# Five more weight pairs by seven block products, and the last expert group in halves of the columns

## The reference

```python
# layer 1
u = rms_norm(h, norm_pre_mix)
proj = u @ w_in                                   # 17 slabs of 512 columns
y_a = hgrn2_mixer(hq, hf, hi, hg, ...)            # gated linear recurrence
y_b = nsa_mixer(nq, kc, vc, ks, vs, kw, vw, ...)  # attention in three branches
merged = sigmoid(ga) * (y_a @ w_branch_a) + sigmoid(gb) * (y_b @ w_branch_b)
h = h + rms_norm(merged @ w_out)
h = h + rms_norm(square(relu(rms_norm(h) @ w_up)) @ w_down)
h = h + rms_norm((p @ w_ple) * sigmoid(h @ w_ple_gate))
# layer 2: two kinds of sparse attention, then 32 experts, 2 for each token
x = x + mixed @ w_out
x = x + hier_moe(rms_norm_2(x, g_ffn), ...)       # w1, w3: 1024x512, w2: 512x1024 each
return rms_norm_2(x, g_final)
```

## Time and profile before

| what | value |
| --- | --- |
| median of 3 runs | 1384.84 us (1382.62 to 1387.03) |
| the profiled execution's own time | 1382.68 us |
| its span | 1380.9 us |
| PE busy | 1172.0 us (85%) |
| DVE busy | 473.2 us (34%) |
| ACT busy | 253.4 us (18%) |
| POOL busy | 143.7 us (10%) |
| read from HBM | 328.64 MB |

### The profile page before, as it was taken

How to read it: one execution, slowest core, us unless ns; L and a number is a source line. 1 busy time by engine, 2 the same in 40 slices (tenths; PEclk the granted TensorE clock), 3 DMA queues, 4 the chain that set the end, 5 groups by cost and what they waited for, 6 DMA issues and landing times. The chain is left out here.

```text
span 1380.9 us, 14269 instructions
## 1 busy us (share of the span) xinstructions
PE 1172.0 (85%) x6095; PEld 669.0 (48%) x6095; DVE 473.2 (34%) x778; ACT 253.4 (18%) x497; POOL 143.7 (10%) x159
## 2 busy tenths in 40 slices
PE   7999999999999999999999999997656365564745
PEld 7946655556855999444544446452212031221311
DVE  7672333025615554545683542231001010010102
ACT  2331003125701211001312275021000000000001
POOL 1011004010110225420032000100000000000000
PEclk9999999999999999999999999999888787887878
DMA  9641223351115444444444110998999999999994
GB/s 388 241 182 62 84 100 122 127 239 62 62 61 231 175 152 183 149 166 172 146 174 177 67 35 28 384 405 334 428 428 429 426 429 427 428 429 427 428 424 171
DMA packets 26981, 330.68 MB, mean 239 GB/s; under 512 B 4112, under 2 KB 4896, under 8 KB 6176
## 3 DMA queue, kind: packets, MB, share of 16 engines
q1 hardware_dynamic: 26912, 329.70, 59.1%
HBM read 328.64 MB, written 1.05 MB: 239 GB/s over the span
## 5 line engine op out<-in xcount | busy, mean ns | idle before, releaser
L227 PE MATMUL ps<-ring,arena 128*128 128x512 f32 (+2 forms) x1880 | 685.9, 621 | 91.2 <-DMA ring<-in_w 51.0
L227 PE MATMUL ps<-arena 128*128 128x128 f32 (+9 forms) x2706 | 513.6, 419 | 75.3 <-DMA ring<-in_w 21.4
L227 PEld LDWEIGHTS ps<-ring,arena 128*128 128x128 f32 (+2 forms) x1880 | 260.7, 164 | 405.4 <-issue 399.0
L227 PEld LDWEIGHTS ps<-arena 128*128 128x128 f32 (+3 forms) x2706 | 290.1, 171 | 224.1 <-issue 189.6
L1930 DVE TENSOR_TENSOR arena<-ps,junk 128x512 f32<-128x512 f32 x8 | 5.5, 691 | 367.5 <-PE ps L227 367.5
L227 PE MATMUL ps<-misc,arena 128*32 128x512 f32 (+3 forms) x216 | 84.4, 553 | 22.7 <-DMA arena<-in_w 22.7
L227 PE MATMUL ps<-arena,ring 128*128 128x128 f32 x768 | 88.2, 275 | 0.0
L227 PEld LDWEIGHTS ps<-arena,ring 128*128 128x128 f32 x768 | 87.0, 192 | 0.5 <-issue 0.5
L230 PE MATMUL ps<-cst,arena 128*128 128x128 f32 x456 | 60.5, 277 | 5.2 <-ACT arena L473 2.0
L230 PEld LDWEIGHTS ps<-cst,arena 128*128 128x128 f32 x456 | 51.8, 142 | 26.5 <-issue 16.6
L366 DVE TENSOR_TENSOR arena<-ring 128x2048 f32<-128x2048 f32 (+1 forms) x19 | 36.8, 1936 | 39.6 <-PE ps L227 39.5
(11 more groups left out here) (268 smaller groups left out, 638.5 us busy)
## 6 DMA issues: line engine op xcount, KB each, us to landing
arena<-in_w SPq DMA_DIRECT2D x42, 2048.0 KB, 35.4
ring<-in_w SPq DMA_DIRECT2D x42, 2048.0 KB, 33.9
ring<-in_w_in SPq DMA_DIRECT2D x27, 2048.0 KB, 7.9
ring<-in_w_up SPq DMA_DIRECT2D x8, 2048.0 KB, 8.3
ring<-in_w_down SPq DMA_DIRECT2D x8, 2048.0 KB, 7.7
misc<-in_w SPq DMA_DIRECT2D x8, 2048.0 KB, 34.6
ring<-in_w_out SPq DMA_DIRECT2D x4, 2048.0 KB, 14.5
ring<-in_w_branch_a SPq DMA_DIRECT2D x2, 2048.0 KB, 10.0
```

What stands on the lines that cost most here:

```text
L227: return lambda q: q.matmul(out_, l, r, start=s, stop=e, skip_group_check=skip)
```

## The change

Five pairs of slabs of layer 1 are now multiplied by seven block products instead of 32 plain matmuls: w_in 8 and 9, 10 and 11, 13 and 14, 15 and 16, and the pair of w_branch_a. The work is cut into seven steps of one product each (`pair_steps`), in the order of products 1, 2, 3, 5, 7, 6, 4, and the sums of the weights are written over the weights themselves. A step counts as half a filler, so that `fill(1)` gives two steps, and the loop over the chunks takes two steps for one half before. w_in 12 keeps the plain form. The token sums and the temporaries stay in the ring's fifth buffer, so that the ring has four until w_out, the first slab in the fifth again. w_out waits until all engines are past the attention. The factor 0.125 of the queries moves from their evacuation to their transposes.

In the last expert group the second halves of the w2 slabs come in two loads of 512 KB each, the second four all behind the first four, and the matmuls on them in two parts. `combine` and the closing work are done by halves of the columns. The residual is added by four matmuls with the identity on PE, behind `combine` of the group before, and the squares are taken from PSUM.

```diff
+        s_tail = sem("s_tail")
...
-        order, loads, at_slab = list(range(NR)), [0] * len(ring), {"n": 0}
+        order, loads, at_slab = list(range(NR - 1)), [0] * len(ring), {"n": 0}
...
+        def pair_steps(srcs, S_of, tmp, put):
...
+            def go(n, B, *tokens):
+                P, i = unit()
+                a, ta = S_of(n)
+                t = pe.group([mm(P[:, 0:512], a[:, c, :], B[:, c, :], c == 0, c == 3) for c in range(4)], ta, list(tokens), unit_users[i])
...
+            def copied(o, i, t, dst, *tokens):
+                unit_users[i] = act.op(lambda q: q.activation(dst, o, ACT.Copy), t, list(tokens))
...
+            def weight(name, out_, a, b, *tokens):
+                h[name] = dve.op(lambda q: q.tensor_tensor(out_, a, b, ALU.subtract), list(tokens))
...
+            def first():
...
+                o, i, t = go(1, h["B11"], t0)
+                h["x"] = copied(o, i, t, x, step_free["t"])
+                weight("T1", h["B11"], h["B12"], h["B11"], t, t1)
...
+            def second():
+                o, i, t = go(2, h["B21"], h["t0"])
+                unit_users[i] = h["c11"] = put(0, 0, lambda d, *g: dve.op(lambda q: q.tensor_tensor(d, o, x, ALU.add), t, h["x"], list(g)))
+                weight("T3", h["B12"], h["B22"], h["B12"], h["T1"])
...
+            def third():
+                o, i, t = go(3, h["B22"], h["t1"])
+                h["y"] = copied(o, i, t, y, step_free["t"])
+                weight("T2", h["B22"], h["B22"], h["B11"], t, h["T1"], h["T3"])
+                weight("T4", h["B21"], h["B21"], h["B22"], h[2], h["T2"])
...
+            def fifth():
+                o, i, t = go(5, h["B11"], h["T1"])
+                h["z"] = copied(o, i, t, z, step_free["t"])
+                h["yz"] = pool.op(lambda q: q.tensor_tensor(y, y, z, ALU.add), h["y"], h["z"])
...
+            def sixth():
+                o, i, t = go(6, h["B22"], h["T2"])
+                done(h["k"][1], [t, h[7], h["T4"]])
+                unit_users[i] = h["u"] = dve.op(lambda q: q.tensor_tensor(u, o, x, ALU.add), t, h["x"], step_free["t"])
+                h["c12"] = put(0, 1, lambda d, *g: dve.op(lambda q: q.tensor_tensor(d, y, u, ALU.add), h["yz"], h["u"], list(g)))
+                h["uv"] = pool.op(lambda q: q.tensor_tensor(v, v, u, ALU.add), h["u"], h["zv"])
+                h["c22"] = put(1, 1, lambda d, *g: pool.op(lambda q: q.tensor_tensor(d, z, u, ALU.add), h["u"], h["zv"], list(g)))
...
+            def fourth():
+                o, i, t = go(4, h["B21"], h["T4"])
+                done(h["k"][0], [t, h[5], h["T2"]])
+                unit_users[i] = h["c21"] = put(1, 0, lambda d, *g: dve.op(lambda q: q.tensor_tensor(d, o, v, ALU.add), t, h["uv"], list(g)))
...
+            return [(0.5, f) for f in (first, second, third, fifth, seventh, sixth, fourth)]
...
+        scratch = [ring[NR - 1][:, j * 512:j * 512 + 512] for j in range(8)]
+        SA = [four(v) for v in scratch[0:4]]
...
+        nsa_steps = pair_steps([w_in[8], w_in[9]], lambda n: SX[n], tmp5, put_nq) + pair_steps([w_in[10], w_in[11]], lambda n: SX[n], tmp5, put_kv)
+        nsa_steps += whole(halves(w_in[12], XT, 8, t_u, scaled(KV[:, :, 1024:1536], 1.0, kv_toks, t_rsb)))
...
-                nsa_steps.pop(0)()
+                nsa_steps.pop(0)[1]()
+                nsa_steps.pop(0)[1]()
...
-        fillers = gate_steps(lambda i: w_in[13 + i], GA, None, ga_t, t_yat)
+        gate_free = [t_yat]
+        fillers = gate_pair([w_in[13], w_in[14]], lambda n: SX[n], tmp5, GA, ga_t, gate_free)
...
+            while fillers and n > 0:
+                size, step = fillers.pop(0)
+                step()
+                n -= size
...
+        fill(0.5)
...
-        fillers += gate_steps(lambda i: w_in[15 + i], GB, None, gb_t, [flat, t_yat])
+        fillers += gate_pair([w_in[15], w_in[16]], lambda n: SX[n], tmp5, GB, gb_t, [flat, t_yat])
...
-        fillers += weigh_steps(lambda i: A["w_branch_a"][i], YAT, 8, t_yat, GA, ga_t, None, mg_t)
+        SY, tmp6 = {}, {(0, 0): HB, (0, 1): tmp5[2], (1, 1): tmp5[1], (1, 0): tmp5[3]}
...
+        def put_a(m, n, add):
+            o, g = tmp6[m, n], GA[:, m, n * 512:n * 512 + 512]
+            r = add(o)
+            mg_t[m].append(pool.op(lambda q: q.tensor_tensor(g, g, o, ALU.mult), r, ga_t[m]))
+            return r
...
+        fillers += [(0, begin_a)] + pair_steps([A["w_branch_a"][0], A["w_branch_a"][1]], lambda n: SY[n], tmp5, put_a)
...
+        slab_users[NR - 1] = scratch_free
+        x = at_slab["n"] % (NR - 1)
+        order[:] = [NR - 1] + [(x + y) % (NR - 1) for y in range(NR - 1)]
...
+            W, tok, k = slab(A["w2_2"][e][:, 2048:3072], 2)
+            W = ring[k][:, 0:2048]
+            last_parts.append(lambda: sp.dma(W[:, 1024:2048], A["w2_2"][e][:, 3072:4096], s_tail, 64))
...
-                    W = [[deep_half(e, n) for e in es] for n in range(2)]
+                    W = [[deep_half(e, 0) for e in es], [deep_quarters(e) for e in es]]
...
+                    two_steps = k == NG - 1 and n == 1
+                    for cc in ((0, 1), (2, 3)) if two_steps else ((0, 1, 2, 3),):
...
+                        combine(k, (n,))
+                        closing(n)
...
+            def add_residual():
+                return pe.group([mm(OUTS[m][:, n * 512:n * 512 + 512], ident, X[:, m, n * 512:n * 512 + 512], False, False)
...
+                    fin_sq[m, n] = act.op(lambda q, m=m: q.activation(junk[:, n * 512:n * 512 + 512], OUTS[m][:, cs], ACT.Square, scale=D ** -0.5,
...
+                if k == NG - 1:
+                    t_res = add_residual()
...
-            combine(NG - 1)
...
-                    fo[m].append(dve.op(lambda q, m=m, cs=cs: q.tensor_tensor(X[:, m, cs], OUTS[m][:, cs], X[:, m, cs], ALU.add), cbn[n]))
-            final(X, fo)
+            close()
```

More of the change, by code:

```diff
@@ L468, in gate_steps, with whole, gate_pair, put @@
+        def whole(steps):
+            return [(1, f) for f in steps]
+        def gate_pair(srcs, S_of, tmp, Gd, got, guard):
+            def put(m, n, add):
+                o = Gd[:, m, n * 512:n * 512 + 512]
+                r = add(o, *guard)
+                got[m].append(act.op(lambda q: q.activation(o, o, ACT.Sigmoid), r))
+                return r
+            return pair_steps(srcs, S_of, tmp, put)
         def gate_steps(src, Gd, r, got, guard):
@@ L596, in build @@
         T1 = [four(U(x)) for x in (10, 11, 12)]
-        S, sums = token_sums(dve, XT, [four(U(13)[:, j * 512:j * 512 + 512]) for j in range(4)], t_u[0], t_u[1], None)
+        scratch = [ring[NR - 1][:, j * 512:j * 512 + 512] for j in range(8)]
+        SA = [four(v) for v in scratch[0:4]]
+        S, sums = token_sums(dve, XT, SA, t_u[0], t_u[1], None)
         sums()
-        def four_of(x):
-            return [U(x)[:, j * 512:j * 512 + 512] for j in range(4)]
+        SX = S
+        tmp = scratch[4:8]
         def next_in(a, free):
@@ L701, in build @@
         nxt = next_in(0, {})
-        t = seven(job, S, four_of(6), None, True, put_f, nxt)
+        t = seven(job, S, tmp, None, True, put_f, nxt)
         job, nxt = nxt, next_in(4, {})
@@ L1182, in build @@
         tap("yb", U(11), ob_tok[0], ob_tok[1])
-        while fillers:
-            fillers.pop(0)()
+        fill(99)
+        scratch_free = [pe.now(), act.now(), dve.now(), pool.now()]
         P, i = unit()
@@ L1544, in build @@
         ga_t, gb_t, mg_t = [[], []], [[], []], [[], []]
-        fillers += gate_steps(lambda i: w_in2[7 + i], GA2, SC3, ga_t, pe.now())
+        fillers += whole(gate_steps(lambda i: w_in2[7 + i], GA2, SC3, ga_t, pe.now()))
         for m in range(2):
@@ L1577, in build @@
             t_dm.append(dve.op(lambda q, dm=dm, cmk=cmk: q.tensor_tensor(dm, dm, cmk, ALU.min), t))
-        fillers += gate_steps(lambda i: w_in2[9 + i], GB2, SC3, gb_t, t_dm)
+        fillers += whole(gate_steps(lambda i: w_in2[9 + i], GB2, SC3, gb_t, t_dm))
         fill(2)
```

93 lines of the change are left out of this document (67 added, 26 removed).

## The result

The change makes the kernel slower: 1402.82 us (median of 4 runs, 1401.60 to 1403.75) against 1385.93 us for the kernel before (4 runs), a ratio of 1.0124 with a 95% interval of 1.0109 to 1.0138. That is 16.9 us, where 3.8 were forecast and 10 were the top of the range. The profiled execution took 1403.09 us with a span of 1401.3 us, 20.4 us over that of before; the profile of before is of an execution of 1382.68 us, near the fastest, so the traces differ by more than the medians.

The account below looks back on a forecast made before the run. PE was taken to bound the stretches before the experts, transfers those from 945 us. Terms -6.4 + 8.2 + 3.5 - 1.2 - 0.3 gave +3.8 us, a median of 1388.6 us; range 1384 to 1391, with rivals 1376 to 1395.

Parts of the forecast that it names:

- The reading of what bounds the kernel: Whole kernel: transfers hold everything from 945 us; before the experts, a microsecond of PE moves the expert stage by as much.
- The matmuls: All five pairs: 28 matmuls for 32, 3.43 us less per pair, -17.2 us if PE never waited.
- The recurrence: Two pairs in the chunk loop: -6.9 us of matmuls, +0.5 us for the norm behind chunk 4, -6.4 us.
- From the keys to the attention: Two pairs, first filler to first attention job: -6.9 us of matmuls, waits of 3.4, 2.9, 1.8 and 7.0, +8.2 us.
- The clock: Keys to first attention job: half clock behind the first two waits, about 1.75 us each, +3.5 us, bounds 0 and 8.8.
- The attention: w_branch_a's pair: -3.4 us of matmuls, next scores 2.2 us late behind POOL's four sums, -1.2 us.
- The end: Last expert group: PE, not the last transfer, sets the end; only the smaller last output is won, -0.3 us.
- What was called hidden: Loads with a ring of four and w_out's late load stay covered; a lost cover would show 4.9 us.
- The first: Rival, all five pairs: DVE and POOL shut each other out, +5 us on the forecast, 1393.6 us; chance 0.38.
- The forecast's own mechanism: Keys to attention: PE waits for copies and flats standing behind the pairs' sums on DVE and POOL; forecast 1388.6 us, chance 0.44.
- The second rival: Cover holds, half of 15.1 us new idle and most clock cost fall away: about 1376 us, 1367 without any; chance 0.18.
- the third: Rival, last group: PE reaches the last quarters before they land, end up to 3 us shorter; within the forecast's class.

Follow-up runs that it names:

- the filled waits: Useless 128x512 matmuls put in five waits of PE, against the kernel with only the two pairs of w_in 13 to 16 as block products: 1395.19 us, 7.8 us below it.
- the gates' kernel: Only the pairs w_in 13/14 and 15/16 as block products, other pairs plain, against the kernel before: 1402.96 us, ratio 1.0126.
- the kernel with the copies ahead: Only pairs w_in 13 to 16 as block products, with copies, flats and clearings issued ahead of their sums, against the kernel before: 1379.73 us, ratio 0.9964.
- e9_residual_early: Changed kernel with w_branch_a plain, copies and clearings issued ahead of the sums, residual's matmuls moved to group 1, against the kernel before: 1372.55 us, ratio 0.9917.

## Why the prediction was wrong

**The reading of what bounds the kernel** was right: a microsecond lost ahead of the experts moved the end by as much. The offset is 19.6 us at 403 us and 20.4 at the end.

**The matmuls.** Right as a count: 28 for 32 at 0.86 us each, in every stretch. Of the 6.9 us of the recurrence's pairs 3.3 were left, in the trace and in the kernel that has only them.

**The recurrence**, -6.4 us forecast, -3.3 measured. The wait for chunk 4's norm was placed rightly and mis-sized. The step that failed is "+0.5 us". It took the second sum at 0.7 us and counted 0.5. ACT's square is given DVE's last instruction to wait for (`dve.now()`), so all of the second sum lay on the path, and beside POOL's sum it took 1.79 us, 1.1 more: 1.87 us of wait. The prediction also had nothing for the clock there ("PE back to back"), and the row behind took 1.6 us more. -6.9 + 1.9 + 1.6 = -3.4.

**From the keys to the attention**, +8.2 forecast without the clock. Term by term: ks 3.4, measured 2.88; kw 2.9, measured 3.15; flats 1.8, measured 1.70. These three were right (the terms as listed for kw and the flats add up to 2.7 and 1.6). For the compressed branch the sum has 7.0 us of new idle: the waits are 2.73 + 3.92 + 1.49 + 0.78 + 1.41 = 10.3 us, less the 2.1 that stood there before, so 8.2. The size is near by luck, since its inner working was wrong: the copy `w2d`, on POOL behind the sum y+z, isn't in the list at all, although it is the same mechanism as kw's; and the wait was forecast behind ACT's copy while the largest is at the scores, behind the clearing of VB, which is given ACT's last instruction to wait for, the sigmoid of c22. By the idles alone the stretch would be -6.9 + 18.1 - 2.1 = 9.1 us longer, close to the forecast.

**The clock** is the term that made the prediction wrong. It had +3.5 us, for the first two waits. In the trace these two kept the clock, and the later ones lost it: 20.4 - 9.1 = 11.3 us of the stretch are slower matmuls. Rows that both traces have show 10.6 of them: 17.00 us for 14.19, 1.11 for 0.55, 9.73 for 7.03, 3.65 + 3.62 for 5.44, and a step of 6.27 for 3.60. The failing sentence is "The waits of the compressed branch lie ahead of a step with slack behind it, and add nothing". There was little slack: PE's matmuls were on the path again, since DVE's sums that end the chains waited for the slow rows at 291.35 and 311.92 to end:

```profile
301.12 0.69 DVE L520 TENSOR_TENSOR misc<-ps,ring 128x512 f32<-128x512 f32 x1 [9.06 <-PE ps L228]
318.23 0.69 DVE L528 TENSOR_TENSOR arena<-ps,ring 128x512 f32<-128x512 f32 x1 [2.50 <-PE ps L228]
```

Even the bound named for five waits, 8.8 us, was too low. That the clock is a cause and no by-product is shown by the filled waits, 7.8 us.

**The attention**, -1.2 forecast, +2.4 measured. The wait for POOL's four sums was forecast at 2.2 us and took 1.91. Missing were 1.73 us for ACT's copy behind the exponentials, and the clock: -3.4 + 1.9 + 1.7 leaves 2.2 us for it, of which the two rows behind the wait of 1.91 us show 1.7 (1.96 us for 1.09 and 4.46 for 3.60).

**The end**, -0.3 forecast, +0.3 in the trace. That PE and not the transfers set it was right, and the early residual shows it with 3.75 us.

**What was called hidden** was hidden: without pairs the kernel is not slower, and in the changed kernel PE waits for no transfer up to 440 us.

**The rivals.** The first, with DVE and POOL excluding each other, had the sign. The case that it named came about, y+z of the pair 13/14 began at 244.66 while T4 ran, but the price was small: 0.3 us for each y+z (1.57 and 1.56 us for 1.27), 0.2 for the copy of kw (0.80 for 0.61), 0.45 for c22 ahead of the clearing (1.72 for 1.27) and 1.1 in the recurrence, some 2.3 us in all. In the attention one POOL product took 3.25 us beside a weight sum, and nothing waited for it. Moving the sums off POOL in the mended kernel gained nothing. The forecast's own mechanism, work that stands or waits behind the sums, with a larger price for the clock, gave the result. The rule of the Trainium skill that was weighed against the forecast holds, and decided little. The second rival, a cover that holds, is out, since each wait forecast there stood in the trace; so is the third, since PE and not a load was late at the end.

With the slower rows as measured in the three stretches, 11.3 + 1.6 + 2.2 us for the 3.5, the forecast would have come to 1388.6 + 11.6 = 1400.2 us. The range had to reach there: it ended at 1395.

## What to carry to other kernels

When filler work on the matrix engine is replaced by filler work that also uses the other engines, list for each of their queues what is issued behind the new instructions and who waits for it, the clearings and small copies too; then issue ahead whatever doesn't depend on the new work. Look as well for waits on "the last instruction given to an engine": new work makes them later, whether it has to do with them or not. Here the two together were worth some 23 us, with the same arithmetic. Price a wait of the matrix engine at its length plus a slower stretch behind it, each time it occurs on the path (here behind waits from 0.87 us on, and not behind each), and keep the spread of that as part of the range.

## What was not expected of the hardware

- The clock's fall is not a function of the wait. Behind 2.88 and 3.15 us of idle it stayed at 1.00 in the changed kernel, behind 1.70 us it was at 0.57. Behind the same 3.15 us the gates' kernel lost it: its next 16 records took 8.73 us for 7.03. The same 1.72 us cost 0.1 us in the next row of one kernel's trace and 2.7 us in another's, and behind 0.87 us the next row took 3.62 us in the kernel with the copies ahead and 1.97 in e9_residual_early. One kernel's runs spread from 1383.0 to 1392.3 us with mean clocks of 0.937 and 0.932, where the one of 1372.55 us stayed within 1.6 us in five runs. Few waits alone don't explain that: the kernel without pairs spread over 5.3 us in twelve. What makes the spread isn't shown.
- The clock also fell without an idle of PE. In the kernel with the copies ahead, the compression took 15.79 us for 14.19, with PE busy throughout:

```profile
254.00:258.00 4.00, 4.00 (x34) 3.68 (x32) 0.69 (x1) 1.55 (x3) 0.87 (x1) 0.99 0.61 176
258.00:262.00 4.00, 4.00 (x23) 2.31 (x24) 0.00 (x0) 1.59 (x3) 0.00 (x0) 0.59 1.04 438
262.00:266.00 4.00, 4.00 (x40) 2.53 (x38) 0.00 (x0) 0.00 (x0) 0.00 (x0) 1.00 0.97 414
```

In the kernel with the filled waits the same happened at the same place, behind the small projection and with no idle of PE:

```profile
264.00:268.00 4.00, 4.00 (x11) 1.39 (x12) 1.70 (x7) 1.59 (x3) 0.00 (x0) 0.57 0.99 422
```

In the mended kernel of 1372.55 us the compression took 14.19 us behind the same projection. The cause stays open: no run was made for it.
